# Values and first gates as block products, gates as 1 + tanh(z/2), in a two-layer encoder kernel

## The reference

```
h = rms_norm(x)
aq, ak, av, bq, bk, bv, cq, ckv, ckr, gates = split(h @ w_in)
oa = rms_norm(differential attention(aq, ak, av))      # A: 4 heads
ob = dilated attention(bq, bk, bv)                     # B: 8 heads
oc = latent attention(cq, ckv, ckr)                    # C: 8 heads, rotary keys
x += sum_n( sigmoid(gates_n) * (o_n @ w_branch_n) ) @ w_out      # n = A, B, C
x += cross attention(rms_norm(x), rms_norm(mem))       # 256 memory tokens
x += mixture of experts(rms_norm(x))                   # 32 experts, two per token
```

## Time and profile before

| | before |
|---|---|
| median of 3 runs | 1635.29 us (1633.64 to 1635.59) |
| profiled execution, its own time | 1631.88 us |
| its span, first to last instruction | 1630.0 us |
| TensorE busy | 1321.4 us (81%) |
| TensorE weight loads busy | 800.7 us (49%) |
| VectorE busy | 616.0 us (38%) |
| ScalarE busy | 265.0 us (16%) |
| DMA, mean | 309 GB/s |

### The profile page before, as it was taken

The page is one execution under the profiler, slowest core; times in us unless marked ns, Lnnn a source line. Parts: engine busy times, 40 slices in busy tenths (PEclk is TensorE's granted clock), DMA queues, the critical chain, the costliest instruction groups (busy, mean ns, idle before and its releaser), DMA issues. The chain is left out here.

```text
span 1630.0 us, 20117 instructions
## 1 busy us (share of the span) xinstructions
PE 1321.4 (81%) x8362; PEld 800.7 (49%) x8362; DVE 616.0 (38%) x1159; ACT 265.0 (16%) x659; POOL 33.5 (2%) x46
## 2 busy tenths in 40 slices
PE   7999999999666566677689999999997666666666
PEld 6986689855122122233269757996642211312211
DVE  5655478644211211221163563974531111111121
ACT  2224411032010000000021344110400000000002
POOL 2000000001000000000000000000100000000000
PEclk9999999999887888798899999999998787788778
DMA  9762035849999999999988321476799999999997
GB/s 306 255 203 65 27 108 190 352 178 348 413 421 421 422 413 422 421 421 421 421 294 268 118 66 56 129 261 256 255 386 421 422 421 421 395 421 421 420 421 288
DMA packets 143921, 504.02 MB, mean 309 GB/s; under 512 B 9424, under 2 KB 83216, under 8 KB 96720
## 3 DMA queue, kind: packets, MB, share of 16 engines
q1 hardware_dynamic: 140224, 494.41, 77.6%
q0 software_dynamic: 1712, 4.04, 0.9%
q10 hardware_dynamic: 1888, 4.19, 0.7%
HBM read 501.56 MB, written 1.05 MB: 308 GB/s over the span
## 5 line engine op out<-in xcount | busy, mean ns | idle before, releaser
L2211 PE MATMUL banks<-ring,v 128*32 128x512 f32 x1888 | 295.8, 758 | 175.8 <-DMA ring<-in_w_dram 164.4
L2211 PEld LDWEIGHTS banks<-ring,v 128*32 128x32 f32 x1888 | 78.7, 135 | 379.4 <-issue 377.0
L2279 PE MATMUL banks<-ring,probT 128*32 128x512 f32 x960 | 145.7, 731 | 80.6 <-DMA ring<-in_w_dram 73.8
L2279 PEld LDWEIGHTS banks<-ring,probT 128*32 128x32 f32 x960 | 38.0, 131 | 171.8 <-issue 163.0
L1511 DVE COPY q<-banks 128x512 f32<-128x512 f32 x16 | 11.1, 692 | 240.1 <-PE banks L2279 208.4
L1875 PE MATMUL banks<-hT,ring 128*128 128x256 f32 x416 | 93.3, 382 | 0.5 <-ACT kx_wide L895 0.5
L1973 PE MATMUL banks<-hT,ring 128*128 128x128 f32 x768 | 89.9, 275 | 0.7 <-ACT hT L821 0.7
L1973 PEld LDWEIGHTS banks<-hT,ring 128*128 128x128 f32 x768 | 88.1, 192 | 2.0 <-issue 1.7
L1507 DVE TENSOR_TENSOR q<-banks,q 128x512 f32<-128x512 f32 x16 | 11.1, 692 | 202.6 <-PE banks L2211 202.6
L1875 PEld LDWEIGHTS banks<-hT,ring 128*128 128x128 f32 x416 | 77.9, 190 | 14.6 <-issue 3.3
L2160 PE MATMUL banks<-v,h 128*128 128x128 f32 x512 | 65.9, 289 | 18.5 <-issue 17.8
(11 more groups left out here) (383 smaller groups left out, 1661.7 us busy)
## 6 DMA issues: line engine op xcount, KB each, us to landing
ring<-in_w_dram SPq DMA_DIRECT2D x348, 1024.0 KB, 19.1
ring<-in_w_in_dram SPq DMA_DIRECT2D x52, 1024.0 KB, 8.6
ring<-in_w_branch_dram SPq DMA_DIRECT2D x8, 1024.0 KB, 4.8
ring<-in_w_out_dram SPq DMA_DIRECT2D x8, 1024.0 KB, 9.1
ring<-in_w_dram SPq DMA_DIRECT2D x16, 512.0 KB, 14.2
shared<-in_w_dram SPq DMA_DIRECT2D x6, 1024.0 KB, 6.5
ring<-in_w_branch_dram SPq DMA_DIRECT2D x8, 512.0 KB, 3.6
k<-in_w_dram SPq DMA_DIRECT2D x4, 1024.0 KB, 10.8
```

The lines of the kernel that those rows point to most:

```text
L2211: last = nc.tensor.matmul(bank[2 + m][e * CAP:(e + 1) * CAP, :], xt[:, k, e * CAP:(e + 1) * CAP], ws[e](r), start=k == 0, stop=k == KD - 1)
L2279: last = nc.tensor.matmul(bank[6 + half][e * CAP:(e + 1) * CAP, :], hiddenT[:, k, e * CAP:(e + 1) * CAP], ws[e](2 * r + half), start=k == ...
```

## The change

- A's values become a fifth early block product (NE = 5), by token: its stationary operand is a block of hT and 256 weight columns move. The jobs av0 and av1 go; c0, c1, c2 and bv0 move to steps 0, 2, 4 and 6.
- All twelve gates are computed in six late block products. The first two of them are cut into pieces that TensorE does at the end of steps 19 to 25 (PIECES); the jobs g0 to g3 go. Their sums are made by VectorE in steps 16, 17, 20 and 21, the differences (make_halves) in step 19, the joins in steps 22 and 26.
- After the steps: branches 0, block product 3, branches 1, block products 4 and 5, branches 2, block product 6, branches 3.
- A block product uses two banks (all but the first): p1, p6, p2, p7, q5, p4, q3, in turn one bank and the other.
- A gate is tanh(z/2) by ScalarE; mix multiplies (1 + tanh) with the branch product in one scalar_tensor_tensor, and the factor 1/2 comes in where the output projection is added to x. The additions and reciprocals go.
- The ring has six turns more per layer (64 ahead of the experts instead of 58), and EMPTY is 8. The tile for k0 is loaded after the last mix and after eight ring tiles.
- VectorE makes vx ahead of the first differences in layer 0, and the first sum of layer 1 ahead of copy_hT. The first block product runs p1, q5, p6, p2, p7, q3, p4.

```diff
+PARTS = ("p1", "p6", "p2", "p7", "q5", "p4", "q3")
+FIRST_PARTS = ("p1", "q5", "p6", "p2", "p7", "q3", "p4")
-EARLY_DOUBLES = ("aq", "ak", "bq", "bk")
+EARLY_DOUBLES = ("aq", "ak", "bq", "bk", "av")
+GATE_DOUBLES = [(2 * _i, 2 * _i + 1) for _i in range(6)]
+DOUBLE_BANKS = [(0, 2, 1), (5, 6, 5), (7, 3, 7), (2, 4, 2), (5, 6, 5),
+                (0, 1, 0), (1, 0, 1), (5, 6, 5), (2, 3, 2), (4, 5, 4), (7, 2, 7)]
+PIECES = {19: (0, ("p1", "p6")), 20: (0, ("p2", "p7")), 21: (0, ("q5", "p4", "q3")),
+          22: (1, ("p1", "p6")), 23: (1, ("p2", "p7")), 24: (1, ("q5", "p4")), 25: (1, ("q3",))}
-FILL = {0: ["av0"], 1: ["av1"], 3: ["c0"], 5: ["c1"], 7: ["c2"],
-        8: ["bv0", "kr"], 9: ["cs"], 10: ["bv1"], 11: ["cq0"], 12: ["cqr", "cq1"], 13: ["ck0", "cr"],
-        14: ["ck1"], 16: ["cv0"], 17: ["cv1"], 18: ["g0"], 19: ["as0", "as1"],
-        20: ["g1"], 22: ["g2"], 24: ["g3"]}
+FILL = {0: ["c0"], 2: ["c1"], 4: ["c2"], 6: ["bv0"], 8: ["kr"], 9: ["cs"], 10: ["bv1"], 11: ["cq0"],
+        12: ["cqr", "cq1"], 13: ["ck0", "cr"], 14: ["ck1"], 16: ["cv0"], 17: ["cv1"], 19: ["as0", "as1"]}
...
@@ SP
-                wait_free(sp, l, DOUBLES[-1] + SUM_HIGH)
-                load_beside(l, 0)
...
-                quad_turns(0, in_ring[:RING])
+                quad_turns(0, in_ring[:RING - 4])
+                sp.wait_ge(mix_sum, l * 4 + 5)
+                load_beside(l, 0)
+                quad_turns(0, in_ring[RING - 4:RING])
...
@@ ScalarE, step i, after its jobs
+                    if i in PIECES:
+                        copy_double(l, NE + PIECES[i][0], PIECES[i][1])
+                    if i == 24:
+                        tanh_double(l, NE)
                     if LAG_T <= i < X0 + LAG_T:
                         copy_probsT(i - LAG_T)
...
@@ VectorE
             for l in range(DEPTH):
+                if l > 0:
+                    sum_double(l, 0, (0,))
                 copy_hT(l)
+                if l == 0:
+                    mem_values(0)
                 dve.wait_ge(hT_act, l * COPIES + 2)
                 dve.wait_ge(hT_dve, l * COPIES_DVE + 2)
-                prepare_double(l, 0)
+                first_sums(l)
+                sum_double(l, 1)
                 if l == 0:
-                    mem_values(0)
                     set_up_tables()
...
                 for i in range(X0 + LAG_OUT + 1):
+                    if i == 19:
+                        dve.wait_ge(pv_done, l * PRODUCED + C0 // 2)
+                        make_halves(l, 1)
+                    if i == 22:
+                        join_double(l, NE)
+                    if i == 26:
+                        join_double(l, NE + 1)
                     if i >= LAG_OUT and (i - LAG_OUT) % 2 == 1:
                         copy_out(l, (i - LAG_OUT) // 2)
                     if i < X0:
                         maxima(l, i)
...
                         weigh(l, i - 1)
+                    if i in (16, 17):
+                        sum_double(l, NE, ((0, 1), (2, 3))[i - 16])
+                    if i in (20, 21):
+                        sum_double(l, NE + 1, ((0, 1), (2, 3))[i - 20])
+                    if i == 24:
+                        sum_double(l, NE + 2)
...
@@ mix
-                    nc.vector.tensor_tensor(es[n], bank[BRANCH_BANK[pair, n]][:, :], es[n], ALU.mult).then_inc(mixed, 1)
+                    nc.vector.scalar_tensor_tensor(es[n], es[n], 1.0, bank[BRANCH_BANK[pair, n]][:, :], ALU.add, ALU.mult)\
+                      .then_inc(mixed, 1)
...
@@ TensorE
+            def wait_bank_free(l, n, b):
...
+                elif n == NE:
+                    wait_copied(pe, l, ("as1", "as0")[b])
...
                     if i >= LAG_PV and (i - LAG_PV) % 2 == 1:
                         products(l, (i - LAG_PV) // 2)
+                    if i in PIECES:
+                        double(l, NE + PIECES[i][0], PIECES[i][1])
```

More of the change, by code:

```diff
@@ L1357, in job, with halves_made_by, make_halves @@
                 last.then_inc(copied["dve"], 1)
-            def prepare_double(l, n):
+            def halves_made_by(l, late, count):
+                return l * 8 + 4 * late + count
+            def make_halves(l, late):
+                to = late_halves if late else early_halves
+                a11, a12, a21, a22 = (hT[:, 4 * k:4 * k + 4, t * P:(t + 1) * P] for t in range(2) for k in range(2))
+                nc.vector.tensor_tensor(to[0], a21, a22, ALU.subtract).then_inc(halves_made, 1)
+                dve.wait_ge(halves_made, halves_made_by(l, late, 1))
+                nc.vector.tensor_tensor(to[1], to[0], a11, ALU.subtract).then_inc(halves_made, 1)
+                dve.wait_ge(halves_made, halves_made_by(l, late, 2))
+                nc.vector.tensor_tensor(to[2], a12, to[1], ALU.add).then_inc(halves_made, 1)
+                nc.vector.tensor_tensor(to[3], a11, a21, ALU.subtract).then_inc(halves_made, 1)
@@ L1397, in join_double @@
-                dve.wait_ge(double_made, (l * ND + n) * DOUBLE_MADE + 4)
-                dve.wait_ge(double_joined, done + 1)
-                nc.vector.scalar_tensor_tensor(high[:, :, 0:P], double_bank(n, 2), s, high[:, :, 0:P], ALU.mult, ALU.add)\
-                  .then_inc(double_joined, 1)
-                dve.wait_ge(double_copied, copies + 4)
-                nc.vector.tensor_tensor(high[:, :, P:], high[:, :, P:], low[:, :, P:], ALU.subtract)\
-                  .then_inc(double_joined, 1)
@@ new lines, in join_double @@
+                wait_double_copied(dve, l, n, "p7")
+                nc.vector.tensor_tensor(c22, c22, c21, ALU.subtract).then_inc(double_joined, 1)
+                wait_double_copied(dve, l, n, "q5")
+                dve.wait_ge(double_joined, done + 2)
+                nc.vector.tensor_tensor(c22, c22, double_spare(n), ALU.add).then_inc(double_joined, 1)
+                wait_double_made(dve, l, n, "p4")
+                nc.vector.scalar_tensor_tensor(c21, double_bank(n, "p4"), s, c21, ALU.mult, ALU.add).then_inc(double_joined, 1)
@@ L1410, in maxima @@
+                wait_double_made(dve, l, n, "q3")
+                nc.vector.scalar_tensor_tensor(c12, double_bank(n, "q3"), s, c12, ALU.mult, ALU.add).then_inc(double_joined, 1)
             def maxima(l, i):
@@ L1671, in add_projected @@
                     xs = x[:, t, half * 512:half * 512 + 512]
-                    nc.vector.tensor_tensor(xs, xs, bank[(SUM_BANKS, CROSS_BANKS)[n - 1][o]][:, :], ALU.add).then_inc(x_added, 1)
+                    if n == 1:
+                        last = nc.vector.scalar_tensor_tensor(xs, bank[SUM_BANKS[o]][:, :], 0.5, xs, ALU.mult, ALU.add)
+                    else:
+                        last = nc.vector.tensor_tensor(xs, xs, bank[CROSS_BANKS[o]][:, :], ALU.add)
+                    last.then_inc(x_added, 1)
                 dve.wait_ge(xcol_in, 48 + l * 32)
@@ L2123, in products @@
                 pe.wait_ge(probsT_copied, l * NI + (2 * u + 2))
-                for first, names in ((A0, ("av0", "av1")), (B0, ("bv0", "bv1")), (C0, ("cv1",))):
+                for first, names in ((B0, ("bv0", "bv1")), (C0, ("cv1",))):
                     if 2 * u == first:
@@ L2319, in _ @@
                     double(l, n)
-                job(l, JOB_NAMES[0])
                 if l == 0:
```

468 lines of the change are left out of this document (242 added, 226 removed).

## The result

The changed kernel takes 1641.31 us in the median of 5 runs (1639.83 to 1644.62), the kernel before 1635.29 (1633.64 to 1636.24): ratio 1.0040, 95% interval 1.0025 to 1.0054. It is slower by 6.0 us; the forecast was 1638.3. The two profiled executions lie 8.0 apart: span 1638.0 with 1.8 around it, against 1630.0 in the table of before.

What follows compares the result with a forecast made beforehand. TensorE bounds the kernel up to the experts, which run at DMA's pace. Terms -10.1 - 5.5 - 0.7 - 1.0 + 6.0 + 11.0 and clock +3.3 give +3.0, so 1634.9; plus 3.4 to the median, 1638.3 us; range 1628 to 1645.

Steps and rivals of the forecast that it cites:

- the clock falls at step 9 too: Rival, chance 0.14: the clock also falls behind the waits at step 9, +6.3, giving 1641.6 us.
- TensorE work: Values and four gates as block products: -1.77 and -3.26 us per layer, -10.1 for both layers.
- Start of layer 0: Cross values moved ahead of the first sums: TensorE's wait for vx goes, first block product ends at 40.6, -5.5 us.
- Layer 1's first sum: First sum made ahead of the transposed copies in layer 1: TensorE's wait of 0.66 goes, -0.7 us.
- The tail of layer 0: Six more ring turns: layer 1's weights asked for later, shortening the last expert tiles' distance; 0 to -1.0, taken as -1.0.
- Step 9: First attention: with fewer fillers TensorE waits 0.8 and 3.0 at cs, before 0.74; +3.0 per layer, +6.0 us.
- Third attention: Steps 16 to 25: added VectorE work and ScalarE copies bring waits of 6.4 against 0.9; +11.0 us for both layers.
- The clock: Lower TensorE clock behind the two waits at step 19, 1.65 each: +3.3 us, ends 0 and +6.6; none charged at step 9.
- Tables: Table loads for tanh at steps 20, 23, 24: 0 to +1.3 us per layer, taken as 0.
- Experts: The experts run at DMA's pace, and their stage shifts one for one with the TensorE event before it.
- the attention steps take the VectorE work in: Rival, chance 0.24: VectorE's idle time absorbs sums and differences at maxima(19), wait falls to 2.1, clock stays; 1629.3 us.
- DMA was late: Rival, chance 0.07: last block weights' slots and k0's tile start the experts late, +2.5 us per layer, 1643.3.

Runs made afterwards that it cites:

- best2: Changed kernel with fillers at steps 1, 3, 5, 8, differences behind maxima(19), logarithms at step 18, probability copies ahead of pieces, fold and normalization ahead of kr and bv1: 1617.62 us.
- before_vx: Kernel before with one edit alone: in layer 0 VectorE copies the cross values ahead of the first product's differences and sums; 1632.00 us, ratio 0.9993.
- fill: Changed kernel with filling products c0, c1, c2 at steps 1, 3, 5 and bv0 at step 8, instead of 0, 2, 4, 6; 1635.12 us, ratio 1.0004.
- sums_early: Changed kernel with the four sums of the first gate product in steps 13 and 15 instead of 16 and 17; 1643.38 us, ratio 1.0055.
- halves_late: Changed kernel with the four VectorE differences of step 19 behind maxima(19) instead of ahead of it; 1633.86 us, ratio 0.9997.
- logs_early: Changed kernel with ScalarE reordered: square of oa in step 15, as0 and as1 with logarithms in step 18, turned probabilities copied ahead of pieces; 1628.53 us, ratio 0.9972.
- vx_late: Changed kernel with the cross values of layer 0 copied behind the first and second products' sums again; 1655.11 us, ratio 1.0128.
- tanh_only: Kernel before with the gates alone written as 1 + tanh(z/2), without add and reciprocal on VectorE; 1634.15 us, ratio 0.9999.
- warm_cs: Changed kernel with 12 needless products on TensorE right ahead of its wait for VectorE at cs of step 9; 1639.27 us, ratio 1.0030.

## Why the prediction was right, and where its terms were off

The time lies in the range of 1628 to 1645, and the waits came up at the places and with about the lengths that I had given. The size did not: I forecast +3.0, at the bound of what I called no change, and gave no change 0.39 and slower 0.37; measured is +6.0. The median lies 3.0 above the forecast, on the rival "the clock falls at step 9 too" (1641.6). Against the two profiles, which lie 8.0 apart, the sum is short by 5.0. Its numbers, with best2 as the measure of the same work without lost clock:

- *TensorE work*: 280.4 - 276.3 = 4.1 per layer, not 5.03; -8.1, not -10.1. The values gave 1.9: the chain before has av0 with 6.91 and av1 with 7.10, and 12.09 stands in their place. The gates gave 2.1 and not 3.26, counted from start to next start: the four plain ones took 27.9 and not 28.40, their fourteen pieces in best2 25.9 and not 25.14, since nine of them, at the edge to other work, take 1.88 and five 1.79 (in after: 193.06 to 194.94, 200.37 to 202.16). That product lengths hold when cut into pieces was a wrong assumption.
- *Start of layer 0*: 5.0 (block product 0 ends at 41.17, before at 46.15), 5.5 predicted. Right in size, but I gave it to the place of vx alone; before_vx shows that it needs the second sums ahead of the tables as well.
- *Layer 1's first sum*: the 0.66 is gone, and VectorE made that sum without a wait for weights, as predicted.
- *The tail of layer 0*: the distance over the last expert tiles fell from 10.98 to 10.03 (815.83 to 825.86), as predicted, but nothing was won by it: from layer 0's output projection to layer 1's first block product it is 519.5 before and 519.7 after, since the wait at 815.83 came 1.5 later, counted from the projection. So +0.3, not -1.0.
- *Step 9*: 0.93 + 2.72 - 0.74 = 2.9, 3.0 predicted.
- *Third attention*: 0.80 + 3.46 + 1.05 and some tenths; 1.3 + 3.6 + 1.1 + 0.3 predicted. Together with step 9 idle time grew by 6.7 + 0.7 (the sum that went) = 7.4 per layer, 8.5 predicted: +14.8, not +17.
- *The clock*: 279.8 - 276.3 = 3.4 per layer, of it 1.6 behind cs and 1.3 behind the first piece (0.5 I can't place): +6.8, not +3.3. This term was furthest off. I charged the wait of 3.46 and not that of 2.72, as if length decided; in the traces of both layers both fell.
- *Tables*: none is loaded for tanh; the one for the logarithms takes 1.28 and they start 0.01 behind its end, as in the earlier trace rows. The Trainium skill (ScalarE: Activation LUTs, Table sets: the hidden batching unit) puts tanh in exp's set; by that rule, the trace agrees.
- *Experts*: from the projection of layer 1 to the end of the span it is 511.6 before and 511.4 after, so they shifted one for one, as assumed.

Of the rivals, "the attention steps take the VectorE work in" fell with the first row of step 19, and DMA was late nowhere: gates and branches kept their length with the loads moved, and so did the experts. The sum by measured terms is -8.1 - 5.0 - 0.7 + 0.3 + 14.8 + 6.8 - 0.2 (the experts of layer 1) = +7.9, the 8.0 of the two profiles. The medians lie only 6.0 apart: the profiled execution of before (1631.88) is faster than every run behind its median (1633.64 to 1636.24). That the forecast is nearer to the medians than to the profiles is luck; so is it that idle time, put 2.2 too high, hid a part of what clock, work and tail were short by.

The change itself was worth most of what it promised: work, start and sum make 8.1 + 5.0 + 0.7 = 13.8, where I had 17.3 with the tail. best2 keeps all of it and is 16 faster (13.4 to 18.5 by its interval); its steps also wait 0.5 per layer less than those of before (1.52 against 137.20 - 135.14 = 2.06). The new order of best2 alone was not tried in the kernel before; by these 2.06, all at full clock, it could gain 4.1 there at most. In the changed kernel the gain was taken back in the attention steps, by the places of the fillers, the differences, the logarithms and the copies of turned probabilities.

## What to carry to other kernels

Work taken out of the engine that sets the end helps only so far as its partners keep up: follow the other engines' queues step by step with the new spacing, and ask of every late item what stands ahead of it and whether that must. A wait that ends on one engine is often a chain over two; look for the cheaper end to cut, and for buffers that forbid an earlier start, before moving work. Put a price on a long wait of TensorE that is its length and a clock loss on top, and keep two ends for the latter: behind waits of 2.72 to 3.74 it was 1.3 to 3.0 here in 22 of 24 stretches, and nothing in two; behind waits up to 1.49 it was nothing.

## What the runs showed that I had not expected

*The same wait costs between nothing and 3 us of clock.* The wait of 2.72 at cs stands in six traces, two layers each. From the start of cs to that of the job of step 11 it is 11.38 in before and in fill, where a wait of 0.74 stands ahead. Behind 2.72 it is 11.38 once (sums_early, layer 0), 12.93 to 12.99 nine times, and 14.43 and 14.36 in layer 0 of halves_late and logs_early: a loss of 0, 1.6 or 3.0. From the start of the first gate piece to the turn of step 24 it is 30.80 in halves_late (wait 1.49). Behind waits of 3.46 to 3.74 it is 30.80 once (sums_early, layer 0), 1.3 to 1.6 more six times and 2.6 to 2.8 more five times. This stretch of sums_early, against that of halves_late behind an equal wait:

```profile
132.20:135.60 3.40, 3.37 (x15) 1.00 0.02 5
```

```profile
131.70:135.60 3.90, 3.87 (x9) 0.50 0.02 4
```

I did not find what decides it. The length of the wait does not: these are equal waits of the same instructions. Nor does the spread of the times tell: sums_early spans 1639.03 to 1646.12 over 5 runs, but vx_late, with the same waits, 1654.66 to 1655.63 over 4.

*A stall without a releaser, in patterns that differ between kernels.* Among the experts TensorE stands still 5 to 7 us with no semaphore to wait for, near the point where a flag is read. In before, then in after:

```profile
598.72 5.85 PE L2160 MATMUL banks<-v,h 128*128 128x128 f32 x32 [7.22 <-issue]
...
1389.55 0.80 PE L2160 MATMUL banks<-v,h 128*128 128x128 f32 x2 [5.81 <-issue]
1395.08 5.01 PE L2160 MATMUL banks<-v,h 128*128 128x128 f32 x30 [4.74 <-issue]
```

```profile
598.38 0.58 PE L2248 MATMUL banks<-v,h 128*128 128x128 f32 x1 [6.01 <-issue]
604.10 5.35 PE L2248 MATMUL banks<-v,h 128*128 128x128 f32 x31 [5.14 <-issue]
...
1399.89 5.35 PE L2248 MATMUL banks<-v,h 128*128 128x128 f32 x32 [5.81 <-issue]
```

The pattern one and two is that of before, tanh_only and before_vx; two and one that of after and of all variants of it but warm_cs, which has one and one. With one trace of each kernel, this suggests that the pattern belongs to the program and not to the execution, but doesn't show it. The queue of instruction transfers is active there; that these are late instructions is argued, not shown. Counted from the layer's output projection, TensorE's last restart comes 3.5 later in after than in before in layer 0 and 3.4 earlier in layer 1, so the effect nearly cancels over both.
